# Feed-forward matmuls regrouped: high and part of the low activations in one 512-column step

## What is computed

```python
def conv_ffn(h, buf, w_up, w_gate, conv_w, conv_b, w_down):
    L = h.shape[1]
    up = h @ w_up
    gate = h @ w_gate
    ext = jnp.concatenate([buf.astype(gate.dtype), gate], 1)
    act = jax.nn.gelu(causal_dwconv(ext, conv_w, L) + conv_b)
    return (act * up) @ w_down, ext[:, -(FFN_CONV - 1):]
...
x = x + y
y, fb = conv_ffn(rms_norm(x, p['norm_ffn'][l]), ffn_buf[l], p['w_up'][l], ...)
x = x + y
```

## Time and profile before

| | us |
|---|---|
| median of 3 runs | 2832.09 (2831.94 to 2833.06) |
| profiled execution, its own time | 2830.86 |
| its span in the trace | 2829.0 |
| TensorE busy | 2807.9 (99%) |
| VectorE busy | 1555.0 (55%) |
| ScalarE busy | 1032.5 (36%) |
| DMA, mean rate | 149 GB/s |

### The profile page before, as it was taken

One profiled execution on the slowest core, in us unless ns is written; L12 is line 12 of the kernel. 1 busy time (PEld: TensorE's weight loads), 2 busy tenths in 40 slices (PEclk: granted clock), 3 DMA queues, 4 the chain that ended last, 5 costly groups with the idle time before them and its releaser, 6 DMA issues.

```text
span 2829.0 us, 49617 instructions
## 1 busy us (share of the span) xinstructions
PE 2807.9 (99%) x19055; PEld 2794.4 (99%) x19055; DVE 1555.0 (55%) x2178; ACT 1032.5 (36%) x1135; POOL 123.6 (4%) x136
## 2 busy tenths in 40 slices
PE   9999999999999999999999999999999999999998
PEld 9999999999999999999999999999999999999998
DVE  7666645554355543555666566455554455535554
ACT  5444333333233333333444443443333333323333
POOL 0000021000000000002200000220000000000012
PEclk9999999999999999999999999999999999999999
DMA  6444444444444444444444444444444444444443
GB/s 237 146 144 137 133 150 143 158 142 156 149 149 147 150 151 149 148 152 150 138 137 149 137 149 142 146 148 150 148 151 150 151 148 149 149 149 149 149 149 114
DMA packets 120785, 420.26 MB, mean 149 GB/s; under 512 B 13689, under 2 KB 19841, under 8 KB 120577
## 3 DMA queue, kind: packets, MB, share of 16 engines
q1 hardware_dynamic: 120128, 418.45, 44.6%
q10 hardware_dynamic: 576, 0.66, 0.1%
HBM read 412.92 MB, written 6.14 MB: 148 GB/s over the span
## 4 chain that ended last, share of the span: by engine, by line
PE 98%; DVE 1%; ACT 0%; DMA 0%; issue 0%; DVEq 0%; ACTq 0%
PE gb L463 95%; PE ab L469 3%; PE ab L482 1%; DVE w_lo L1097 0%; DMA x<-in_x 0%; PE ab L663 0%; DVE work L1731 0%; DVE work L1225 0%; ACT w_hi L785 0%; DVE rt L1727 0%; DVE work L1189 0%; DVE a_lo L1104 0%; DVEq L140 0%; ACT a_hi L840 0%; ACT a_hi L792 0%
## 5 line engine op out<-in xcount | busy, mean ns | idle before, releaser
L1097 DVE TENSOR_TENSOR w_lo<-raw,w_hi 128x1024 fp32r<-128x1024 f32 x767 | 943.2, 1230 | 1183.0 <-ACT w_hi L785 1180.9
L785 ACT ACTIVATE w_hi<-raw 128x1024 fp32r<-128x1024 f32 x769 | 814.6, 1060 | 1663.6 <-PE gb L463 1661.3
L463 PE MATMUL gb<-a_hi,w_hi 128*128 128x320 f32 x4216 | 1311.5, 311 | 0.2 <-DVE a_lo L1104 0.2
L463 PE MATMUL gb<-a_hi,w_lo 128*128 128x320 f32 x4216 | 1303.1, 309 | 0.0
L463 PE MATMUL gb<-a_lo,w_hi 128*128 128x320 f32 x4216 | 1303.0, 309 | 0.0
L463 PEld LDWEIGHTS gb<-a_hi,w_hi 128*128 128x128 f32 x4216 | 792.1, 188 | 2.0 <-DVE a_lo L1104 0.4
L463 PEld LDWEIGHTS gb<-a_lo,w_hi 128*128 128x128 f32 x4216 | 792.0, 188 | 1.2
L463 PEld LDWEIGHTS gb<-a_hi,w_lo 128*128 128x128 f32 x4216 | 791.7, 188 | 0.0
L463 PE MATMUL gb<-b_hi,w_hi 128*128 128x320 f32 x1920 | 593.7, 309 | 0.0
L463 PE MATMUL gb<-b_hi,w_lo 128*128 128x320 f32 x1920 | 593.3, 309 | 0.0
L463 PE MATMUL gb<-b_lo,w_hi 128*128 128x320 f32 x1920 | 593.3, 309 | 0.0
(11 more groups left out here) (182 smaller groups left out, 809.0 us busy)
## 6 DMA issues: line engine op xcount, KB each, us to landing
raw<-in_weights SPq DMA_DIRECT2D x769, 512.0 KB, 3.3
out_y<-work SPq DMA_DIRECT2D x4, 640.0 KB, 3.0
out_c<-work SPq DMA_DIRECT2D x8, 257.0 KB, 5.6
x<-in_x SPq DMA_DIRECT2D x3, 640.0 KB, 6.9
work<-m_scratch SPq DMA_DIRECT2D x8, 192.0 KB, 5.0
work<-in_ret_tables SPq DMA_DIRECT2D x8, 160.0 KB, 3.3
work<-in_ml_state SPq DMA_DIRECT2D x8, 128.5 KB, 5.2
work<-in_w_pool SPq DMA_DIRECT2D x1, 1024.0 KB, 7.1
```

The lines of the kernel that those rows point to most:

```text
L463: last = nc.tensor.matmul(bank(b, m), w[:, at:at + P], v[:, t:t + T], start=kg == k == n == 0, stop=kg == groups - 1 and k == UK - 1 and n ...
L785: nc.scalar.activation(w_hi[:, at:at + UW], raw[:, at:at + UW], ACT.Copy).then_inc(hi_ready, 1)
L1097: V.tensor_tensor(w_lo[:, at:at + UW], raw[:, at:at + UW], w_hi[:, at:at + UW].bitcast(F32), ALU.subtract).then_inc(lo_ready, 1)
```

## The change

In both feed-forwards the units of a gate pair and an up pair (or of two pairs of the down projection) alternate, so a group now has four output tiles in all four banks of `gb`. High and low activations of a tile lie side by side in one tensor (`a` and `b` replace `a_hi`, `a_lo`, `b_hi`, `b_lo`), so that 512 consecutive columns are the 320 high ones and the first 192 low ones.

For one block of weights there are now two matmuls where there were three: high weights by those 512 columns (the low ones sum in columns 320 to 511 of the bank), and low weights by 320 high columns. The last 128 low tokens are taken the other way round for a group's four output tiles at once: they are the stationary operand, and 512 high weights move (`left_of`, one matmul for each input tile). Their sum is token-major in a bank of `ab`; ScalarE copies it to `left` (`save_left`), and a matmul with an identity turns it and adds it to the four banks (L524, 128 columns each). VectorE adds the 192 low columns when it empties a pair, which is a second instruction on each.

```diff
+WIDE_LO = 512 - T
-        a_hi, a_lo = sb("a_hi", KT * T, F32R), sb("a_lo", KT * T, F32R)
-        b_hi, b_lo = sb("b_hi", KT * T, F32R), sb("b_lo", KT * T, F32R)
+        a, b = sb("a", KT * 2 * T, F32R), sb("b", KT * 2 * T, F32R)
+        left, ident_r = sb("left", 4 * P, F32R), sb("ident_r", P, F32R)
...
+            def left_of(u, q, quads, act):
+                for k in range(UK):
+                    t = (q * UK + k) * 2 * T + T + WIDE_LO
+                    w = w_hi[:, u.slot * UW:(u.slot + 2) * UW].rearrange("p (u k c) -> p u k c", u=2, k=UK)
+                    last = nc.tensor.matmul(left_bank, act[:, t:t + P], w[:, :, k, :], start=q == k == 0,
+                                            stop=q == quads - 1 and k == UK - 1)
+                return last
+            def wide_unit(u, p, q, quads, act, taken, group):
+                pe.wait_ge(lo_ready, u.number(1))
+                if q == 0:
+                    pe.wait_ge(pair_taken, taken)
+                    if p == 0:
+                        pe.wait_ge(left_saved, group)
+                if p == 0 and q == quads - 1:
+                    pe.wait_ge(hi_ready, u.number(2))
+                    left_of(u, q, quads, act).then_inc(left_summed, 1)
+                for m in range(UM):
+                    for k in range(UK):
+                        at, t = u.slot * UW + (k * UM + m) * P, (q * UK + k) * 2 * T
+                        nc.tensor.matmul(gb[:, 2 * p + m, :], w_hi[:, at:at + P], act[:, t:t + 512],
+                                         start=q == k == 0, stop=False)
+                        last = nc.tensor.matmul(bank(p, m), w_lo[:, at:at + P], act[:, t:t + T],
+                                                start=False, stop=False)
+                if p == 0 and q < quads - 1:
+                    pe.wait_ge(hi_ready, u.number(2))
+                    last = left_of(u, q, quads, act)
+                last.then_inc(unit_used, 1)
+                if q == quads - 1:
+                    pe.wait_ge(left_saved, group + 1)
+                    for m in range(UM):
+                        last = nc.tensor.matmul(gb[:, 2 * p + m, WIDE_LO:T], left[:, (2 * p + m) * P:(2 * p + m + 1) * P],
+                                                ident_r[:], start=False, stop=True)
+                    last.then_inc(wide_done, 1)
...
-                    for kg in range(groups):
-                        pe.wait_ge(f_ready, f_base + f // 2 + 2 * kg + 2)
-                        unit(Unit(down_u + kg), kg, groups, b_hi, b_lo, 0, down_p - 1)
+                    for j in range(2 * quads):
+                        q, p = divmod(j, 2)
+                        if p == 0:
+                            pe.wait_ge(f_ready, f_base + f // 2 + 2 * q + 2)
+                        wide_unit(Unit(down_u + j), p, q, quads, b, down_p + p - 1, group)
...
+            def save_left(group):
+                act.wait_ge(left_summed, group + 1)
+                nc.scalar.activation(left[:], ab[:, 1, :], ACT.Copy).then_inc(left_saved, 1)
...
+            def add_wide_to_x(p, b, pairs, taken):
+                dve.wait_ge(wide_done, pairs)
+                step.inc(V.tensor_tensor(two(tiles(x, p * 2)), banks(b), two(tiles(x, p * 2)), ALU.add))
+                own()
+                V.tensor_tensor(two(tiles(x, p * 2))[:, :, 0:WIDE_LO], lows_of(b),
+                                two(tiles(x, p * 2))[:, :, 0:WIDE_LO], ALU.add).then_inc(pair_taken, 1)
+                dve.wait_ge(pair_taken, taken)
```

More of the change, by code:

```diff
@@ L47 @@
 FFN_PAIRS = FT + len(BLOCKS) * KT // UM
+FFN_GROUPS = FFN_PAIRS // 2
 PR_ML = PR_FFN0 + FFN_PAIRS
@@ L657, in gate_unit @@
+                    group += 4
+            ffn(U_FFN0, PR_FFN0, 1, 8, 0, 0)
             def gate_unit(g):
@@ L937, in ffn @@
                             if j == 1:
+                                ffn_gelu(i + g)
+                            if j == 2:
                                 ffn_upper(i + g, i * 2)
                             if j == 6:
-                                ffn_gelu(i + (g + 1))
-                    groups = k // UK
-                    final = b == len(BLOCKS) - 1
-                    for kg in range(groups):
-                        split(Unit(down_u + AHEAD + kg))
-                        if kg == 0:
+                                save_left(i + (group + 1))
@@ L946, in ffn @@
+                    group += k // 2
+                    quads = k // UK
+                    final = n == len(BLOCKS) - 1
+                    for j in range(2 * quads):
+                        split(Unit(down_u + AHEAD + j))
+                        if j == 1:
+                            ffn_gelu(g + k // 2 - 1)
+                        if j == 2:
                             ffn_upper(g + k // 2 - 1, k - 2)
-                    if groups == 4:
+                        if j == 2 * quads - 2:
+                            save_left(group)
@@ L962, in _ @@
-            ffn(U_FFN0, PR_FFN0, 1, 0, "ffn0", "mix1")
+                        with act.Fori(0, 3) as i:
+                            for j in range(8):
+                                split(Unit(down_u + AHEAD + 8 + j, i, 8))
+                                if j == 6:
+                                    save_left(i + (group + 1))
+                    else:
+                        for m in range(1, 4):
+                            for j in range(2 * quads):
+                                split(Unit(down_u + AHEAD + 2 * quads * m + j))
+                                if j in (1, 2):
+                                    done = 2 * m - 3 + j
+                                    if next_weight:
+                                        a_upper(done, next_weight, pair_taken, down_p + done + 1)
+                                    else:
+                                        act.wait_ge(pair_taken, down_p + done + 1)
+                                        z_of(done)
+                                if j == 2 * quads - 2:
+                                    save_left(group + m)
@@ L964, in _ @@
+                    group += 4
+                if next_weight:
+                    a_upper(KT // UM - 2, next_weight, pair_taken, down_p + KT // UM - 1)
+                else:
+                    act.wait_ge(pair_taken, down_p + KT // UM - 1)
+                    z_of(KT // UM - 2)
+            ffn(U_FFN0, PR_FFN0, 1, 0, "ffn0", "mix1", 0)
             H8 = slice(0, HEADS)
@@ L1813 @@
             n = 4 * k
-            weights[at:at + n] = np.stack([gate, up], 1).reshape(n, P, UW)
+            weights[at:at + n] = np.stack([gate, up], 2).reshape(n, P, UW)
             at += n
             n = KT // UM * (k // UK)
-            weights[at:at + n] = units_of(a["w_down"][layer][rows])
+            weights[at:at + n] = units_of(a["w_down"][layer][rows]).reshape(4, 2, k // UK, P, UW)\
+                .transpose(0, 2, 1, 3, 4).reshape(n, P, UW)
             at += n
```

297 lines of the change are left out of this document (168 added, 129 removed).

## The result

The changed kernel takes 2852.41 us (median of 4 runs, 2852.07 to 2852.86). The kernel before, run beside it, takes 2832.26 us. The ratio is 1.0072, 95% interval 1.0059 to 1.0084: slower by 20.2 us, where 9.1 us less had been forecast. The profiled execution has a span of 2851.0 us, 22.0 us more than the 2829.0 before.

The account below looks back on a forecast made before the run. TensorE, busy for 99% of the span, was taken as the bound. -42.2 + 30.5 + 0.8 + 1.8 = -9.1 us took 2830.86 to 2821.8; with 1.2 us for the median, 2823.0 us, range 2806 to 2867.

Parts of the forecast that it names:

- the fixed cost: Feed-forward matmuls on TensorE: each float32r matmul pays 13.3 ns over its columns at any width, so 512 columns cost 226.7 ns.
- The forecast's own sign: Profile after, TensorE: starts of 512-column matmuls 227 ns apart if right, 235 or 216 for the rivals.
- the break-even: Feed-forward matmuls: the price of 512 columns, 228.4 ns, from which the forecast gain of 9.1 us is gone.
- The rate theory: Rival, feed-forward matmuls: float32r columns run at 10/11 of the clock's rate, 512 cost 234.7 ns; 2865 us, chance 0.14.
- dear merging: Rival, merging matmuls: 128 float32r columns take four steps a column, 226.7 ns each; 2854 us, chance 0.06.
- the saving of 42.2 us: Both feed-forwards on TensorE: 3168 fewer matmuls for the same columns, 13.33 ns saved for each.
- Merges: Ends of the feed-forward groups: 272 added matmuls of 128 columns, held by weight loads at 112 ns each, 30.5 us.
- The hidden copies: ScalarE's copy to `left` in each group: ready 2.0 us into a 3.89 us unit, before the merge wants it.
- VectorE's two-step emptying: Emptying a pair within one unit: 1.8 us of work for the first pair, 1.4 us left, so no wait.
- The waits of the last block: Down projection's fifth unit in the last 12 tiles: TensorE waits 0.4 us for VectorE's low part, twice, 0.8 us.
- The end: After the last feed-forward group: matmuls on the last pair's squares start 1.8 us later, held by GpSimd's squares.
- GpSimd's chain: At the end: GpSimd's squares of the pair before the last finish 2.5 us after T, the last unit's end.

Follow-up runs that it names:

- probe: The kernel before, with series of 32 equal-width matmuls added on TensorE after its outputs; whole time not used, float32r of 512 columns reached 226.7 ns.
- the earlier low part: Changed kernel with VectorE making the last product's low part one unit earlier and ScalarE, not GpSimd, squaring the last pair but one: 2850.98 us, ratio 1.0066.

## Why the prediction was wrong

**The failed step** is the price of a 512-column matmul: "I take the fixed cost, 213.3 + 13.3 = 226.7 ns". The row it came from had nothing but 320s in it, one like the other, and I bounded the price by widths only. The price isn't one of the width alone: among 512s it is 226.7 (probe, and 3.63 us for sixteen), in alternation with 320s 233.3 to 234. The forecast's own sign, 227 ns from start to start, was missed by that. Near a `left_of` or a merge it is less, and the 29.2 us that the groups missed are 5.5 ns for each of 5280. The forecast itself had put the break-even at 228.4. The rate theory named nearly the right time for the 512s (234.7) by a mechanism that is refuted, and its 2865 is 13 us off. The rival whose time comes nearest, dear merging (2854), does so by chance: it asks for 226.7 ns a merge, and a pair of merges with what it adds to the 512 behind it is 0.23 us.

**What held.** The number of instructions and the saving of 42.2 us at the forecast's price: with the order changed and nothing else, 17.9 of the missing 29.2 us come back, with longer runs 22.1; some 7 never came. Merges: 112 ns forecast, 105 found by leaving half of them out. The hidden copies and VectorE's two-step emptying: no idle time before L513, L515 or L524 in any group. The waits of the last block: 0.4 us twice forecast, 0.49 - 0.15 = 0.35 us and 0.1 more on the next start measured, gone with the earlier low part.

**What was off in size.** The end: 1.8 us forecast, 3.1 measured (5.8 against 2.7 for the same stretch). GpSimd's chain was right (2.5 us after T forecast, 2.4 measured), but not the clock behind TensorE's pause, which made six matmuls take 3.42 us.

**Where the expected gain went.** 42.2 us saved by fewer matmuls at the forecast's price, 30.5 given back to merges as foreseen, 29.2 to 512s that cost more than that price, 0.9 to the waits and 3.1 to the end: 42.2 - 30.5 - 29.2 - 0.9 - 3.1 = -21.5 us, where the spans differ by 22.0. In the other orders some 7 of the 29.2 stay.

**A slip in the chances.** By its own list the forecast has 0.12 for the same and 0.14 + 0.06 + 0.06 = 0.26 for slower, not 0.13 and 0.25. The sum of the time doesn't use them.

## What to carry to other kernels

A price for a matmul read from a row of equal matmuls holds for a row of equal matmuls. If a change mixes widths of float32r, put those of one width in long runs: here runs of eight were worth 18 us in 2852 and up to sixteen 22. And a short float32r matmul costs about 110 ns (110 at 128 columns, 113 at 192), so splitting work in many of them eats what longer ones save.

## What was not expected of the hardware

- Float32r, 512 alternating with 320: 380.0 ns a pair against 373.3 apart; bfloat16 shows no such thing (351.7 apart, 11.27 / 32 = 352 in alternation). After a change of width the starts are off their value for a while: five 512s behind 320s, nine behind 448s, three 320s behind 512s.
- The surcharge isn't even over the widths: 13.3 ns at 256, 320 and 384 columns, 19.9 at 448, 13.4 at 512 once its run has settled.
- Behind a pause of the same length TensorE's clock differed. Windows of the six float32 matmuls after 2.2 us of idle TensorE: the changed kernel has a granted clock of 0.53 (above), that with runs of eight 0.57, with long runs 0.79, with bfloat16 merges 1.00, the last two here (long runs, then bfloat16 merges):

```profile
2813.90:2816.30 2.40, 2.27 (x6) 1.06 (x6) 0.00 (x0) 0.99 (x4) 0.00 (x0) 0.79 0.00 0
```

```profile
2828.90:2832.40 3.50, 1.88 (x6) 1.06 (x6) 1.01 (x1) 1.43 (x3) 0.00 (x0) 1.00 0.00 0
```

  In the chains they took 3.42, 3.25, 2.28 and 1.90 us. From start to start the float32 matmuls are at 0.53 us from the first on in the changed kernel and from the second with runs of eight; behind a first step of 0.37 they are at 0.27 until the last step with long runs, and to the end with bfloat16 merges: the clock fell at another moment of the same work. What decides it isn't shown; the part of the end's cost that hangs on it, up to 1.5 us, differs between kernels whose instructions on TensorE there are the same.
